# Gathering the experts' rows with products of two rounded halves, and a ring of 15 weight buffers

## What is computed

```python
def expert_choice_ffn(x, w_router, w_gate_up, w_down):
    cap = EC_CAPACITY_FACTOR * T // N_EXPERTS          # 64
    logits = jnp.einsum('btd,de->bte', x, w_router, preferred_element_type=jnp.float32)
    aff = jax.nn.softmax(logits, axis=-1)
    gate, idx = lax.top_k(jnp.swapaxes(aff, 1, 2), cap)
    xs = x[bidx, idx]                                   # the gather
    h = jnp.einsum('becd,edf->becf', xs, w_gate_up)
    hg, hu = jnp.split(h, 2, axis=-1)
    ye = jnp.einsum('becf,efd->becd', jax.nn.silu(hg) * hu, w_down)
    ye = ye * gate[..., None].astype(ye.dtype)
    return jnp.zeros_like(x).at[bidx, idx].add(ye)
```

## Time and profile before

| | |
|---|---|
| median of 3 runs | 2267.78 us (2266.63 to 2267.82) |
| the profiled execution | 2269.32 us |
| its span | 2267.4 us |
| TensorE busy | 2138.1 us (94%) |
| VectorE busy | 1081.3 us (48%) |
| ScalarE busy | 698.2 us (31%) |
| GpSimd busy | 153.4 us (7%) |
| mean granted clock of TensorE | 0.98 of full speed |
| read from HBM | 347.06 MB |

### The profile page before, as it was taken

How to read it: one execution, slowest core, us unless ns; L and a number is a source line. 1 busy time by engine, 2 the same in 40 slices (tenths; PEclk the granted TensorE clock), 3 DMA queues, 4 the chain that set the end, 5 groups by cost and what they waited for, 6 DMA issues and landing times.

```text
span 2267.4 us, 24830 instructions
## 1 busy us (share of the span) xinstructions
PE 2138.1 (94%) x10134; PEld 1537.9 (68%) x10134; DVE 1081.3 (48%) x1551; ACT 698.2 (31%) x1006; POOL 153.4 (7%) x152
## 2 busy tenths in 40 slices
PE   5989999999999999999998998999996999999987
PEld 4768888888777778888887765777785444434333
DVE  7886443445666564434456666555545211112113
ACT  2554322223445442223233454433322000000002
POOL 2221000001000010000010010252000000000000
PEclk9999999999999999999999999999998999999999
DMA  4222223223211122232243121231254798999994
GB/s 167 84 75 90 96 77 119 94 82 112 85 56 61 61 92 95 74 122 93 72 123 122 47 64 56 64 84 66 84 190 173 281 398 354 417 417 417 416 417 194
DMA packets 90832, 350.78 MB, mean 155 GB/s; under 512 B 9152, under 2 KB 19024, under 8 KB 74080
## 3 DMA queue, kind: packets, MB, share of 16 engines
q1 hardware_dynamic: 87616, 342.92, 41.4%
q0 software_dynamic: 2240, 2.71, 0.9%
q10 hardware_dynamic: 864, 3.57, 0.4%
HBM read 347.06 MB, written 2.10 MB: 154 GB/s over the span
## 4 chain that ended last, share of the span: by engine, by line
PE 81%; DVE 9%; ACT 4%; DMA 3%; issue 2%; POOL 0%; SPq 0%; ACTq 0%; DVEq 0%; POOLq 0%
PE PS L1734 18%; PE PS L1736 18%; PE PS L1735 18%; PE PS L2050 8%; PE PS L2086 4%; PE PS L2033 3%; DMA SL<-in_wgu_dram 2%; PE PS L1777 2%; DMA C<-in_wgu_dram 1%; PE PS L1843 1%; DVE XC L1361 1%; PE PS L1857 1%; PE PS L1867 1%; PE PS L2108 1%; PE PS L1991 1%
## 5 line engine op out<-in xcount | busy, mean ns | idle before, releaser
L1734 PE MATMUL PS<-HH,WH 128*128 128x512 f32 x1392 | 561.0, 403 | 36.0 <-DVE HL L1299 21.2
L1736 PE MATMUL PS<-HH,WL 128*128 128x512 f32 x1392 | 547.9, 394 | 0.0
L1735 PE MATMUL PS<-HL,WH 128*128 128x512 f32 x1392 | 547.5, 393 | 0.0
L1295 DVE TENSOR_TENSOR WL<-RAW,WH 128x1024 fp32r<-128x1024 f32 (+5 forms) x300 | 338.8, 1129 | 272.8 <-ACT WH L1048 271.1
L1048 ACT ACTIVATE WH<-RAW 128x1024 fp32r<-128x1024 f32 (+4 forms) x278 | 263.6, 950 | 314.8 <-PE PS L1736 291.2
L1734 PEld LDWEIGHTS PS<-HH,WH 128*128 128x128 f32 x1392 | 264.5, 190 | 113.1 <-issue 30.6
L1736 PEld LDWEIGHTS PS<-HH,WL 128*128 128x128 f32 x1392 | 264.5, 190 | 57.2
L1735 PEld LDWEIGHTS PS<-HL,WH 128*128 128x128 f32 x1392 | 265.0, 190 | 54.8 <-issue 2.0
L2050 PE MATMUL PS<-SL,XS 128*64 128x512 f32 x960 | 228.7, 596 | 9.8 <-DMA SL<-in_wgu_dram 8.0
L2050 PEld LDWEIGHTS PS<-SL,XS 128*64 128x64 f32 x960 | 71.1, 137 | 150.0 <-issue 150.0
L1734 PE MATMUL PS<-MH,WH 128*128 128x512 f32 x352 | 136.9, 389 | 0.0
(11 more groups left out here) (285 smaller groups left out, 2684.9 us busy)
## 6 DMA issues: line engine op xcount, KB each, us to landing
SL<-in_wgu_dram SPq DMA_DIRECT2D x120, 1024.0 KB, 18.4
SL<-in_wdn_dram SPq DMA_DIRECT2D x60, 1024.0 KB, 18.2
RAW<-in_w_dram SPq DMA_DIRECT2D x46, 512.0 KB, 3.4
RAW<-in_wg_dram SPq DMA_DIRECT2D x44, 512.0 KB, 3.4
RAW<-in_wu_dram SPq DMA_DIRECT2D x44, 512.0 KB, 3.3
RAW<-in_wd_dram SPq DMA_DIRECT2D x32, 384.0 KB, 3.1
RAW<-in_wqkv_dram SPq DMA_DIRECT2D x24, 512.0 KB, 3.4
RAW<-in_wd_dram SPq DMA_DIRECT2D x32, 320.0 KB, 3.0
```

Source lines behind the costliest of these rows:

```text
L1295: e.tensor_tensor(wl, raw, wh.bitcast(F), ALU.subtract).then_inc(*wlo.did("u", u))
L1734: e.matmul(out, wh[:, w], xh, start=k == 0, stop=False)
L1735: e.matmul(out, wh[:, w], xl, start=False, stop=False)
L1736: m = e.matmul(out, wl[:, w], xh, start=False, stop=k == g.total - 1)
```

## The change

The gather no longer multiplies `XF` in float32. After the normalised rows of a block are written and turned, ScalarE rounds all 1024 columns of the block into `XH` (fp32r), and GpSimd computes `XL` = `XF` - `XH` (fp32r). `XL` lies at the same addresses as `XF`. The matrix `PE` becomes fp32r as well, which is exact for zeros and ones; where other products read it, they read the same bits as float32. A `gather(q, d)` is now eight products of 256 columns, `XH` and `XL` in turn for the four blocks of rows. The very first gather waits for each block's `XL`.

`XH` needs as much memory as two weight buffers. It comes from one `XS` buffer and one weight buffer: `XS` is now single, so that VectorE writes `XS[:, d, :]` of gather q > 0 only after `up(2q - 1, d)` has read the old one, and `NSLOT` is 15. Group `m` now releases transfers 2m + 15 and 2m + 16. `YOH` and `YOL` move to other addresses.

```diff
-NSLOT = 16
+NSLOT = 15
...
         px = ExitStack()
-        XF = sb("XF", [128, 4, D], F, px)
-        XS = [sb("XS0", [128, DC, 256], F, px), None]
+        pa = ExitStack()
+        XF = sb("XF", [128, 4, D], F, pa)
+        pa.close()
+        XL = sb("XL", [128, 4, D], R, px)
+        XH = sb("XH", [128, 4, D], R, px)
...
-        XS[1] = sb("XS1", [128, DC, 256], F, px)
-        PE = sb("PE", [128, 4, 256], F, px)
+        XS = sb("XS", [128, DC, 256], F, px)
+        PE = sb("PE", [128, 4, 256], R, px)
...
+                elif kind == "x_turn":
+                    tb, = a
+                    e.wait_ge(*tr("xt", tb, 1))
+                    e.wait_ge(*hi("xh", tb))
+                    e.tensor_tensor(XL[:, tb, :], XF[:, tb, :], XH[:, tb, :].bitcast(F), ALU.subtract).then_inc(
+                        *xnl.did(tb))
...
                     e.activation(rows(tb, 0), bank("xt", tb, 0).rearrange("p (c t) -> p c t", c=4), ACT.Copy).then_inc(
                         *xnat.did(tb))
+                    e.wait_ge(*ln("x", 0, tb))
+                    e.activation(XH[:, tb, :], XF[:, tb, :], ACT.Copy).then_inc(*hi.did("xh", tb))
...
                     e.wait_ge(*ex("ga", q, d))
-                    e.tensor_scalar(XS[q % 2][:, d, :], bank("ga", q, d)[:, 0:256], vec("l1g", d), vec("l1b", d), ALU.mult,
+                    if q:
+                        e.wait_ge(*ex("w", 12 * (2 * q - 1) + d))
+                    e.tensor_scalar(XS[:, d, :], bank("ga", q, d)[:, 0:256], vec("l1g", d), vec("l1b", d), ALU.mult,
                                     ALU.add).then_inc(*xs.did(q, d))
...
                     for tb in range(4):
-                        m = e.matmul(bank("ga", q, d)[:, 0:256], XF[:, tb, 128 * d:128 * d + 128], PE[:, tb, :],
-                                     start=tb == 0, stop=tb == 3)
+                        if q + d == 0:
+                            e.wait_ge(*xnl(tb))
+                        cols = slice(128 * d, 128 * d + 128)
+                        e.matmul(bank("ga", q, d)[:, 0:256], XH[:, tb, cols], PE[:, tb, :], start=tb == 0, stop=False)
+                        m = e.matmul(bank("ga", q, d)[:, 0:256], XL[:, tb, cols], PE[:, tb, :], start=False, stop=tb == 3)
                     m.then_inc(*ex.did("ga", q, d))
```

More of the change, by code:

```diff
@@ L860, in program @@
         pa.close()
-        XS[1] = sb("XS1", [128, DC, 256], F, px)
-        PE = sb("PE", [128, 4, 256], F, px)
+        XS = sb("XS", [128, DC, 256], F, px)
+        PE = sb("PE", [128, 4, 256], R, px)
         GT = [sb("GT0", [128, T], R, px), None]
         HG = sb("HG", [128, D], F, px)
-        YOH = sb("YOH", [128, D], R, px)
-        YOL = sb("YOL", [128, D], R, px)
         HT = sb("HT", [128, DC, 128], F, px)
@@ L872, in program @@
         assert CST["bones"] + 2048 <= CST["iota"] and len(SL) == NSLOT
+        YOH = sb("YOH", [128, D], R, px)
+        YOL = sb("YOL", [128, D], R, px)
         GT[1] = sb("GT1", [128, T], R, px)
@@ L2037, in pe_program @@
                     i, k = a
-                    z = (i // 2) % 2
                     if k == 0:
@@ L2049, in pe_program @@
                             x0 = (2 * (i % 2) + e2) * 64
-                            m = e.matmul(bank("h", i, n)[64 * e2:64 * e2 + 64, :], XS[z][:, k, x0:x0 + 64],
+                            m = e.matmul(bank("h", i, n)[64 * e2:64 * e2 + 64, :], XS[:, k, x0:x0 + 64],
                                          SL[(l0 + e2) % NSLOT][:, 512 * n:512 * n + 512], start=k == 0, stop=k == 7)
@@ L2061, in pe_program @@
                                 s0, col = (2 * j + e2) * 64, 16 * tb + 4 * q + 2 * j + e2
-                                m = e.matmul(bank("gw", q)[64 * e2:64 * e2 + 64, j:j + 1], PE[:, tb, s0:s0 + 64],
+                                m = e.matmul(bank("gw", q)[64 * e2:64 * e2 + 64, j:j + 1], PE[:, tb, s0:s0 + 64].bitcast(F),
                                              AF[:, col:col + 1], start=tb == 0, stop=tb == 3, skip_group_check=True)
@@ L2067, in pe_program @@
                     e.wait_ge(*freed("gt", "e", q, j))
-                    pe_turn(e, ("gt", "e", q, j), [PE[:, tb, 128 * j:128 * j + 128] for tb in range(4)])
+                    pe_turn(e, ("gt", "e", q, j), [PE[:, tb, 128 * j:128 * j + 128].bitcast(F) for tb in range(4)])
                 elif kind == "h_turn":
```

## The result

Over four runs each, side by side, the changed kernel takes 2255.41 us (2254.37 to 2256.18) and the kernel before 2267.31 us (2266.63 to 2267.82): a ratio of 0.9947, 95% interval 0.993 to 0.9965, or 11.9 us. The forecast was 2255.3 us.

The account below looks back on a forecast made before the run. The wire carrying weight transfers sets the end, not TensorE. First release -2.6, one buffer less +2.5, regained wire loss -12.9, thin margin +0.5 sum to -12.5 us: 2267.8 to 2255.3 us, 8-in-10 range 2250.5 to 2262.

Parts of the forecast that it names:

- First release: Ahead of group 0: 24 new gather products at the lower clock free the first weight buffer earlier, -2.6 us.
- One buffer: Weight ring of 15: transfer 15 no longer lands before the pause but goes out with the first release, +2.5 us.
- The wire's loss: After the first release, to 1887.4: 12.9 us lost to TensorE's pacing are regained, less 0.5 us for a thin margin.
- the walk: Group-by-group timing from first release: group 19 at 87.9 us, group 20 at 100.4, wire busy until 100.8.
- The rounding: Last rows, before the experts' stage: ScalarE's four roundings and GpSimd's four subtractions cost 0, with 19 us of cover.
- Single `XS`: Experts' stage: VectorE's writes wait for the `up` group of the same step; cost 0, if bare 0.5 us in three pairs.
- The rest turns into waits: Of TensorE's 31 us saved, the rest becomes waits for transfers, some 28 us in place of 9.7.
- TensorE as the bound: Rival: TensorE sets the end and all 31 us are gained, 2237 us; chance 0.02.
- A gather that does not get faster: Rival: gather products stay at 0.24 us, 2270.3 us, or take 0.19 us, 2263 us; chance 0.08 for both.
- The wire paused anyway: Rival: the wire still pauses, half the gain, 2261 us; chance 0.06, shared with a held-up selection chain.
- The selection chain held up: Rival: VectorE's selection is delayed, half the gain, 2261 us; chance 0.06, shared with a paused wire.
- The slower clock: Rival: TensorE's waits of about 1.6 us in pairs 4 to 7 drop the clock to 1.2 GHz, 2284 us; chance 0.04.

Follow-up runs that it names:

- Experiment 3: Changed kernel with every gather step of gathers 2 and 3 done twice (late extra work): 2255.12 us, -11.8 us against the kernel before.
- experiment 1: Changed kernel again, unedited: 2254.3 us, -12.6 us against the kernel before.
- experiment 5: Changed kernel with 13 weight buffers in place of 15: 2259.73 us, -7.8 us against the kernel before.
- experiment 2: Kernel before with 15 weight buffers in place of 16, nothing else changed: 2268.33 us, +1.4 us against the kernel before.
- experiment 4: Changed kernel with every gather step of gathers 0 and 1 done twice (early extra work): 2270.8 us, +3.9 us against the kernel before.
- experiment 9: Kernel before again, unedited, with a profile of its own: 2266.19 us, +0.3 us against the kernel before.
- Experiment 6: Changed kernel plus 54 unused products (49 and 5) keeping TensorE busy during VectorE's selection: 2253.71 us, -13.9 us against the kernel before.
- experiment 10: Changed kernel with gathers in pairs and 58 and 6 unused products on TensorE during the selection: 2252.2 us, -13.7 us against the kernel before.

## Why the prediction was right

Its sum, point by point, against the profiles:

- **The bound** is the wire, as forecast. From 1893 to 2200 it carries 416 GB/s before, after, and in every experiment, and the last `up` group waits 1.3 to 1.4 us for its transfer in each of them. Experiment 3 shows it directly.
- **First release, forecast -2.6.** In the first profile 12.0 -> 9.35 = -2.6; in experiments 1, 3 and 5 -3.7 to -3.8. The forecast assumed the clock to rise behind the 24 products, as it did in the first profile; in the others it rose sooner. Even in the first profile two small errors cancel: the forecast's 0.24 us a product at the lower clock are 0.213 (5.46 us in place of 5.8), and the `up` group behind them takes 3.85 us, not 3.58.
- **One buffer, forecast +2.5.** +2.3 in experiment 2; experiment 5 fits 2.5 a buffer once the clock's 1.4 us are set apart.
- **The wire's loss, forecast -12.9 + 0.5.** The time from first release to last `up` group fell by 441.1 - 433.3 = 7.8 us though it holds one transfer more; so the loss shrank by 7.8 + 2.5 = 10.3 us, where 12.4 was forecast. This is the term that was mis-sized. The step that failed is the gather's 0.96 us: 0.12 us a product came from a row of single-pass products that follow each other, while here each step stands between float32 groups, and both of its ends cost time. The step is 1.15 us. 12 such steps at the full clock, up to group 19, make 12 x 0.19 = 2.3 us, more than the margin of 0.4 us that the walk had found. The rest is the clock at gather 1. The walk had the gather step at the lower clock and the `up` group at the full one, 1.9 + 3.6 us; they took 2.05 + 4.13, which is 0.7 us more. Group 19 ends 1853.88 + 3.58 - 1766.64 = 90.8 us after the first release, where 87.9 was forecast, and group 20's first release comes at 1866.43 + 3.49 = 1869.9, or 103.3, where 100.4 was forecast. The wire needs 100.8 us for the 40 transfers released until then, so 2.5 us are lost. In the other profiles this difference goes with `wire`: 2.8 us are lost in experiment 1 (433.5) and 1.1 in experiment 5 (436.9 with two transfers more).
- **The rounding, forecast 0.** The timelines of GpSimd, of ScalarE and of VectorE around the last rows, and VectorE's in the kernel before:

```profile
1733.78 2.34 POOL L1030 TENSOR_TENSOR XL<-XF,XH 128x1024 fp32r<-128x1024 f32 x1 [3.43 <-ACT XH L1262]
```
```profile
1732.59 1.05 ACT L1262 ACTIVATE XH<-XF 128x1024 fp32r<-128x1024 f32 x1
...
1737.74 0.26 ACT L1265 ACTIVATE AF<-AF 128x64 f32<-128x64 f32 x1 [2.80 <-DVE AF L1650]
```
```profile
1728.16 1.29 DVE L1622 BATCH_NORM_STATS2 BN<-PS 128x6 f32<-128x512 f32 x2 [0.71 <-PE PS L2006]
```
```profile
1732.58 1.30 DVE L1611 BATCH_NORM_STATS2 BN<-PS 128x6 f32<-128x512 f32 x2 [0.71 <-PE PS L1993]
```

  `XH` takes the 1.05 us of the earlier trace rows, `XL` 2.34 where 2.6 was taken; the last ends at 1736.1, 21 us before its use, and ScalarE still waits 2.80 us for `AF` behind it. VectorE's last mean and variance stand ahead of the last rounding; from their start to the first gather product it takes 1757.29 - 1728.16 = 29.13 us now and 1761.75 - 1732.58 = 29.17 before. It takes 29.12 or 29.13 in experiments 1, 3, 4 and 5 (changed) and 29.17 in 2 and 9 (float32 gather). So neither the rounding nor GpSimd's subtractions hold up the selection chain. That the gap of 4.4 us ahead of the stage isn't a gain or a loss of this part follows from this and from the starts in experiment 9 (before, 1758.3) and experiment 5 (changed, 1759.8).
- **Single `XS`, forecast 0.** VectorE's longer waits stand in the page, and no wait of TensorE for an `XS` write stands in either profile. Nothing shows a cost, and no run isolates it.
- **The rest turns into waits, forecast 28 us**: 19.9 us in the first profile (17.2 + 2.7), 17.4 in experiment 1. A step that saves 0.77 us and not 0.96 leaves 32 x 0.19 = 6 us less to wait. The clock at gathers 2 and 3 takes another 3.3 us: a gather step and its `up` group, elsewhere 4.73 us, take 6.41 and 6.35 there (1932.94 to 1939.35 and 2046.18 to 2052.53). Together they explain the 8 us.

Made up from the profile, with the 2.5 us lost until group 20, -2.6 + 2.5 - 12.9 + 2.5 = -10.5 us, against the stage's 10.3. The medians show 11.9 and 12.6. An earlier clock rise, as in experiment 1, gives up to 1.3 us more; that the rest is scatter between executions is not shown. So the mechanism was right, and that the number came so close is in part luck: where the clock rose early, 1.2 us too little on the first release and 2.1 too much on the loss stood against each other.

**The rivals.** TensorE as the bound fell with experiment 3. A gather that does not get faster fell with the profile (1.15 us against 1.93); its second half, a dearer product, was right in a small way: the changes between the kinds are dearer, and not each product. The wire paused anyway fell, but for a rest of 2 us; experiment 4 shows what it would have been like. The selection chain held up fell with the 29.13 us above.

The slower clock fell as a cost. In pair 7, at 14.63 us busy of 20 and waits up to 1.5 us, the clock is 1.00. The Trainium skill, TensorE: Matmul & The Clock Gate, section HAM oscillation, describes products that wait for DMA between bursts, about 3 to 5 us at a time in its example, and fall back to the lower clock; waits of up to 1.5 us in a rhythm of 5 us don't do it here. The prediction read the 2284 us from that section for waits of 1.6 us, which are shorter than those of its example. Experiment 6 agrees with the section in kind: after 2.26 us of idle time the clock was 0.65 of full in the next 4 us.

Yet one sign that the prediction named did come up. It said that a clock below 1.00 in the late pairs would prove it wrong, and from 2040 to 2060, in pair 5, the clock is 0.91. TensorE waits 3.46 us for the one-hot matrix ahead of gathers 2 and 3, in the kernel before as in the changed one. The clock fell behind this wait at gather 2 in all nine profiles with the single-pass gather and at gather 3 in six of them, and in none of the three profiles with the float32 gather. It took time that TensorE had to spare, so the end did not move, and the sign was put too strictly. Which part of the change lets the clock fall there is open.

**Open.** The median moved 1 to 2 us more than the stages of the profiles do; I can't say whether that is all scatter of the clock's rise. In experiments 1, 3, 4 and 5 the stretch from about 1710 to 1722 took 1.5 us longer than in the first profile, with single-pass products at 0.43 us in place of 0.24; the rest of the scatter ahead of the stage lies earlier and was not traced. Why a change between single-pass and float32 products takes 0.1 us was not looked into; in experiment 10 the very first gather product takes 0.20 us by starts too (1757.98 to 1758.18), though single-pass products stand ahead of it. Sixteen buffers beside `XH` and `XL` were not tried.

## What to carry to other kernels

When a transfer queue sets the end, an engine's saving counts only while the queue lacks work: look for stretches in which transfers land soon after their issue, and not at the engine's total. Doubling the same work early and late shows this in two runs. A price from a row of like instructions in a run holds for the run; where they alternate with another kind, price the changes between the kinds apart.

## What was not expected of the hardware

- A row of eight single-pass products of 256 columns takes 0.12 us a product within, and 0.19 us more in all where it stands between float32 products: by starts, 0.10 at its first product and 0.09 on the way back.
- At the lower clock the same product takes 0.213 us, less than twice 0.12.
- The moment at which the clock rises differs by about 1 us between executions of one kernel, and the experts' stage starts up to 3.5 us apart in two profiles of one kernel (1758.27 and 1761.75, before).
- The length of an idle time alone doesn't tell what the clock does. In experiment 6 it fell after 2.26 us without products (0.65 from 1760 to 1764), and in experiment 10 it stayed after 0.29 us. Ahead of gathers 2 and 3, after 3.46 us without products, it stayed 1.00 in the kernel before and fell to 0.91 (2040 to 2060) in the changed one.
